# Two-map attention units: factor and epsilon column on GpSimd, the reciprocal on VectorE

## The reference

```python
logit_d = jnp.einsum('bqhcd,bkhcd->bchqk', dq_b, dk).astype(jnp.float32) * diff_scale
logit_d = jnp.where(allowed[:, None, None], logit_d + bias[:, None], NEG_INF_2)
p_d = jax.nn.softmax(logit_d, axis=-1)
attn_d = p_d[:, 0] - lam * p_d[:, 1]
o_d = jnp.einsum('bhqk,bkhd->bqhd', attn_d.astype(dv.dtype), dv)
o_d = _rms_norm(o_d, diff_sub_norm) * (1.0 - lam_init)
```

## Time and profile before

| | us |
|---|---|
| median of 3 runs | 1720.08 |
| lowest, highest run | 1719.74, 1720.19 |
| the profiled execution, device time | 1719.99 |
| its span in the profile | 1718.2 |
| first reciprocal of the two-map units, start | 1574.51 |
| last reciprocal of the two-map units, start | 1616.50 |

### The profile page before, as it was taken

The page is one execution under the profiler, slowest core; times in us unless marked ns, Lnnn a source line. Parts: engine busy times, 40 slices in busy tenths (PEclk is TensorE's granted clock), DMA queues, the critical chain, the costliest instruction groups (busy, mean ns, idle before and its releaser), DMA issues.

```text
span 1718.2 us, 22179 instructions
## 1 busy us (share of the span) xinstructions
PE 1685.8 (98%) x8825; PEld 1327.9 (77%) x8825; DVE 1029.0 (60%) x1675; ACT 633.9 (37%) x1001; POOL 61.5 (4%) x84
## 2 busy tenths in 40 slices
PE   7999999999999999999999999999999999999999
PEld 6888888787866678668888888888888866677687
DVE  5665444456977755448444457633554587878774
ACT  4222222231257851333222233312222567555730
POOL 0000000000012310000000000000000000002200
PEclk9999999999999999999999999999999999999999
DMA  6645433246300015133433233324332333402322
GB/s 205 204 162 180 135 99 90 69 122 204 94 2 2 2 40 158 61 86 84 107 94 97 85 104 98 91 85 121 88 96 83 100 105 99 127 15 61 100 74 74
DMA packets 233323, 167.60 MB, mean 98 GB/s; under 512 B 10436, under 2 KB 217532, under 8 KB 233092
## 3 DMA queue, kind: packets, MB, share of 16 engines
q1 hardware_dynamic: 230900, 161.98, 32.3%
q10 hardware_dynamic: 2320, 4.20, 0.7%
HBM read 156.31 MB, written 6.30 MB: 95 GB/s over the span
## 4 chain that ended last, share of the span: by engine, by line
PE 89%; DVE 6%; ACT 2%; issue 1%; SPq 1%; DMA 0%; POOL 0%; DVEq 0%; ACTq 0%
PE bank L1065 25%; PE bank L1066 25%; PE bank L1067 25%; PE turned L1314 3%; PE bank L1302 2%; PE bank L1340 2%; DVE bank L2122 1%; PE bank L1496 1%; ACT Pm L820 1%; PE bank L1404 1%; PE turned L1393 1%; PE bank L1622 1%; PE turned L1123 1%; DVE w_lo L1731 1%; SPq L458 0%
## 5 line engine op out<-in xcount | busy, mean ns | idle before, releaser
L1065 PE MATMUL bank<-h_hi,w_hi 128*128 128x512 f32 x1200 | 473.5, 395 | 2.8 <-DVE h_lo L1786 1.5
L1066 PE MATMUL bank<-h_lo,w_hi 128*128 128x512 f32 x1200 | 467.3, 389 | 0.0
L1067 PE MATMUL bank<-h_hi,w_lo 128*128 128x512 f32 x1200 | 467.3, 389 | 0.0
L650 ACT ACTIVATE w_hi<-w_raw 128x2048 fp32r<-128x2048 f32 (+3 forms) x134 | 236.9, 1768 | 495.7 <-PE bank L1067 494.9
L1731 DVE TENSOR_TENSOR w_lo<-w_raw,w_hi 128x2048 fp32r<-128x2048 f32 (+3 forms) x133 | 280.0, 2106 | 63.2 <-ACT w_hi L650 60.6
L1065 PEld LDWEIGHTS bank<-h_hi,w_hi 128*128 128x128 f32 x1200 | 225.3, 188 | 60.2 <-issue 11.8
L1067 PEld LDWEIGHTS bank<-h_hi,w_lo 128*128 128x128 f32 x1200 | 225.3, 188 | 47.4
L1066 PEld LDWEIGHTS bank<-h_lo,w_hi 128*128 128x128 f32 x1200 | 225.3, 188 | 46.6 <-issue 1.0
L1065 PE MATMUL bank<-u_hi,w_hi 128*128 128x512 f32 x352 | 137.1, 389 | 0.0
L1066 PE MATMUL bank<-u_lo,w_hi 128*128 128x512 f32 x352 | 137.0, 389 | 0.0
L1067 PE MATMUL bank<-u_hi,w_lo 128*128 128x512 f32 x352 | 136.9, 389 | 0.0
(11 more groups left out here) (428 smaller groups left out, 2282.1 us busy)
## 6 DMA issues: line engine op xcount, KB each, us to landing
w_raw<-in_w_in SPq DMA_DIRECT2D x28, 1024.0 KB, 5.4
w_raw<-in_ffn_w_gate SPq DMA_DIRECT2D x44, 512.0 KB, 4.0
w_raw<-in_ffn_w_up SPq DMA_DIRECT2D x44, 512.0 KB, 5.3
w_raw<-in_ffn_w_down SPq DMA_DIRECT2D x32, 704.0 KB, 4.7
ada_w<-in_ada_w SPq DMA_DIRECT2D x16, 768.0 KB, 6.5
w_raw<-in_w_in SPq DMA_DIRECT2D x19, 512.0 KB, 4.2
w_raw<-in_w_out SPq DMA_DIRECT2D x8, 1024.0 KB, 5.1
w_raw<-in_w_branch_nsa SPq DMA_DIRECT2D x8, 512.0 KB, 5.8
```

Source lines behind the costliest of these rows:

```text
L650: act.activation(w_hi[s % 2][:, 0:n], w_raw[s % 2][:, 0:n], ACT.Copy).then_inc(s_hi, 1)
L1065: pe.matmul(o, l[0], r[0], start=first, stop=False)
L1066: pe.matmul(o, l[0], r[1], start=False, stop=False)
L1067: return pe.matmul(o, l[1], r[0], start=False, stop=last)
```

## The change

The second and third instruction of `lam_sums` leave VectorE. GpSimd makes them in a new `lam_parts(v)`: first the epsilon column, as soon as the exponentials are there (`p_exp`), then the factor, as soon as VectorE has the reciprocal (`r1_ready`). Both count up `lam_ready`, and the weighing of a two-map unit waits for that instead of `sum_ready`. VectorE no longer waits behind the reciprocal for itself. The mask additions are put between: 0 to 2 as before, then for v = 16 to 31 `lam_parts(v)` and behind it addition v - 13 as long as there is one; these no longer wait for `p_ready`.

```diff
-            for i in range(16):
+
+            def bias_masked(i):
+
                 t = i % 4
                 pool.wait_ge(sem(f"bias_landed{t}"), 16 * (i // 4 + 1))
+                pool.tensor_add(bias[:, t, :], bias[:, t, :], hidden[t]).then_inc(sem("bias_ready"), 1)
+
+            def lam_parts(v):
+
+                u = U0 + v
+                sum0, r1, c1 = mstat[:, u % 2, 4:5], mstat[:, u % 2, 6:7], mstat[:, u % 2, 7:8]
+                pool.wait_ge(sem("p_exp"), u + 1)
+                pool.tensor_scalar(eps_sum(v), sum0, P * EPS, sum0, ALU.mult, ALU.mult).then_inc(sem("lam_ready"), 1)
+                pool.wait_ge(sem("r1_ready"), v - 15)
+                pool.tensor_scalar(c1, r1, sum0, neglam, ALU.mult, ALU.mult).then_inc(sem("lam_ready"), 1)
+
+            for i in range(3):
                 pool.wait_ge(sem("p_ready"), attended(U0 + 13 + i))
-                pool.tensor_add(bias[:, t, :], bias[:, t, :], hidden[t]).then_inc(sem("bias_ready"), 1)
+                bias_masked(i)
+            for v in range(16, len(UNITS2)):
+                lam_parts(v)
+                if v - 13 < 16:
+                    bias_masked(v - 13)
...
                 dve.wait_ge(sem("p_exp"), u + 1)
-                sum0 = mstat[:, u % 2, 4:5]
-                done(dve.reciprocal(mstat[:, u % 2, 6:7], mstat[:, u % 2, 5:6]))
-                tick(dve.tensor_scalar(mstat[:, u % 2, 7:8], mstat[:, u % 2, 6:7], sum0, neglam, ALU.mult, ALU.mult), "sum_ready")
-                tick(dve.tensor_scalar(eps_sum(v), sum0, P * EPS, sum0, ALU.mult, ALU.mult), "dve_seq")
+                tick(dve.reciprocal(mstat[:, u % 2, 6:7], mstat[:, u % 2, 5:6]), "r1_ready")
...
                 if kind == 0:
-                    dve.wait_ge(sem("sum_ready"), attended(u))
+                    dve.wait_ge(sem("lam_ready"), 2 * (v - 15))
                     tick(dve.scalar_tensor_tensor(p0, Pm[u % 2][:, 1, :], mstat[:, u % 2, 7:8], p0, ALU.mult, ALU.add), "p_ready")
```

More of the change, by code:

```diff
@@ L452, in build @@
         swap_used = {**{r: r - 1 for r in range(2, 10)}, **{r: r for r in range(12, 19)}, 19: 20}
+        UNITS2 = [(kind, h, t) for kind in (1, 0) for h in range(4) for t in range(NT)]
+        eps_sum = lambda v: col[:, G_MOD + v - 16:G_MOD + v - 15]
         attended = lambda u: u + 1 - sum(1 for w in UNITS[:u + 1] if w[0] is None)
@@ L610, in tick @@
             return count[name]
-        UNITS2 = [(kind, h, t) for kind in (1, 0) for h in range(4) for t in range(NT)]
-        eps_sum = lambda v: col[:, G_MOD + v - 16:G_MOD + v - 15]
         cq0, dq0, uq0, dkb0, ukv0 = (first_acc[n] for n in ("cq", "dqa", "uq", "dkb", "ukv"))
```

## The result

The changed kernel takes 1721.9 us (median of 20 runs, 1720.2 to 1722.95), the one before 1719.7 beside it (20 runs, 1718.2 to 1720.2): a ratio of 1.0014, 95% interval 1.0008 to 1.002. That is 2.2 us slower: the interval leaves out no change, but the difference is within the 0.2% that were set as the bound.

The account below looks back on a forecast made before the run. In the two-map stage the loop of VectorE and ScalarE, not TensorE, was taken to set the 2.77 us period. Terms 3.9-0.4+0.25+0.24, with roundings +4.1, on 1719.99 gave 1724.1 us; range 1716.3 to 1725.8.

Parts of the forecast that it names:

- main case: Either of two outcomes in the two-map units: addition first, +4.1 us, or weighing first, -3.5 us.
- The forecast case: Two-map units: the mask addition goes before the weighing; +4.1, 1724.1 us, own range 1722.5 to 1725.8, chance 0.57.
- TensorE's floor of 2.54: Two-map units: TensorE's own steps take 0.50, 0.98 and 1.06 us, so no unit can run below 2.54.
- Part 1: VectorE: second score operation moves from T+0.51 to T+0.08, weighing possible at T+0.68; T is the start of a unit's reciprocal.
- Part 2: GpSimd's one-column instructions: epsilon column hidden, factor 0.34 from T+0.26, no cost to the weighing; last unit +0.25.
- Part 3, the mechanism: Two-map units: the addition starts 0.08 before the weighing can, goes first, and the weighing ends about 0.53 behind it.
- Part 3, the start of the addition: GpSimd in two-map units: the mask addition starts right behind the factor, at T+0.60.
- the first score operation follows at +0.05: VectorE in two-map units: next score operation 0.05 behind the weighing's end, next reciprocal 0.62 later, period 3.07 for 2.77.
- The sum: Two-map stage: 3.9 for thirteen units, -0.4 for units 29 and 30, +0.25 end, +0.24 first unit; with roundings +4.1.
- Rival two: Two-map units: the weighing goes first and the addition waits; period 2.54 for 2.77, -3.5, 1716.5 us; chance 0.28.
- ring for GpSimd: GpSimd's unit if the weighing goes first: 0.34+0.34+1.27 and some 0.6 of waiting, 2.55 us.
- Rival three: No change: GpSimd bounds near 2.75 a unit, or the race varies; -1.5 to +1.5, taken as 1720; chance 0.15.

Follow-up runs that it names:

- e2: Changed kernel with mask additions 3 to 15 treating 8 of 512 columns, so part of the masks is missing; 1716.1 us, ratio 0.998.
- e8: Changed kernel with the epsilon column back on VectorE behind the reciprocal, additions 3 to 15 waiting for the next unit's second maximum; 1716.3 us, ratio 0.998.
- e3: Kernel before, with mask additions 3 to 15 waiting for the factor (sum_ready) instead of the weighing (p_ready); 1722.6 us, ratio 1.0016.
- e9: e8 without its added wait, so each mask addition stands directly behind the factor; 1721.9 us, ratio 1.0011.
- e6: Changed kernel with a one-column GpSimd memset between the factor and the mask addition; 1722.4 us, ratio 1.0014.
- e10: Changed kernel with one to four one-column memsets in turn between factor and addition in units 17 to 28, four in unit 16; 1723.3 us, ratio 1.0018.
- e5: Changed kernel with GpSimd's order factor, epsilon column, addition, and the weighing waiting for the factor alone; 1716.4 us, ratio 0.998.
- e11: Kernel before, with the epsilon column between reciprocal and factor in VectorE's order, GpSimd unchanged; 1718.0 us, ratio 0.9986.
- e1: Changed kernel with mask additions 3 to 15 waiting for p_ready again, so they stand behind the weighing; 1721.2 us, ratio 1.0008.

## Why the prediction was right, and where its size was off

The sign and the mechanism came as forecast, and the size at half: +2.2 for +4.1. That 1721.9 lies in the stated range of 1716.3 to 1725.8 says little, since that range reaches from one main case to the other. The forecast case had a range of its own, 1722.5 to 1725.8, and that one was missed by 0.6, on the low side. The result is also inside the 0.2% bound, which had the chance 0.37, and not in the likelier class, slower, with 0.46. The parts one by one:

- **TensorE's floor of 2.54: right.** e2 and e8 run at 2.540, and the score operation of VectorE waits for the scores there.
- **Part 1: right.** The second score operation starts at T+0.075 (said 0.08), and the weighing at T+0.67 (said 0.68), in twelve of twelve units.
- **Part 2: right in size, wrong for unit 16.** The factor starts at T+0.255 and takes 0.340, as said, extrapolated from 128 and 512 columns to one. The epsilon column is done before the factor could start in units 17 to 30 (it ends at T+0.10 at the latest). But in unit 16 the exponentials come late, it starts at T+0.02 and pushes the factor to T+0.38 and the weighing to T+0.76. There I had only the scaling in mind: 3.81 measured for 3.71. The last unit was foreseen: T+0.80 (said about 0.75), +0.30 for +0.25.
- **Part 3, the mechanism: right.** The addition goes first, the weighing waits for the whole of it and needs 0.55 more (said 0.53). e3 shows it without the moved instructions, e2 and e9 against e8 what it costs. That it goes first was given only a little better than even chances. It was no luck of the exact lead: it had 0.12 here and not the 0.08 that was worked out, but e6 and e10 show that it wins with 0.08, with less and with none. The argument by which I gave the addition the first turn, that it reaches its operands sooner since it has no per-partition operand to fetch, is borne out by e10, where it wins from 0.06 behind, and by e5, where a GpSimd instruction with such an operand loses from 0.03 behind. They differ in width and operation too, so that the fetching alone is the reason stays an argument.
- **Part 3, the start of the addition: 0.045 off.** I set it at the factor's end, T+0.60. It starts at T+0.555, 0.04 before the factor's row ends. That makes each period 0.045 shorter.
- **Part 3, the step that was mis-sized: "the first score operation follows at +0.05".** It starts 0.08 before the weighing's end. I had taken the 0.80 from the weighing's start to the next score operation for VectorE's own step. But it was a wait: before, the same operation starts some 0.16 behind the end of TensorE's scores, as the earlier trace rows would have shown one unit on (1589.39+1.13 = 1590.52; e11, with the same order there, has the wait in its rows). The step of VectorE itself stood in the earlier trace rows: the scaling starts at 1576.29, the weighing of before starts at 1575.62 and takes 0.75, so 0.08 before its end. I used that number for unit 16 and the other one for the twelve. This makes 0.13 a unit. In after alone this step and a wait for the scores can't be told apart, as its scores end 0.16 ahead too. But where they end 0.21 to 0.29 ahead the step is still 0.08 before the weighing's end: in all of e3's units 18 to 28, and in e10 (1587.64+1.83 = 1589.47 to 1589.39, with the scores done at 1587.97+1.13 = 1589.10). The trace of before has it once behind a weighing, in unit 17:

```profile
1578.79 0.75 DVE L2437 SCALAR_TENSOR_TENSOR Pm<-Pm,mstat 128x512 f32<-128x512 f32 x1
...
1579.46 0.69 DVE L2122 CUSTOM_DVE_ANT_0 bank<-bank,bias 128x512 f32<-128x512 f32 x1
```

- **The sum.** 0.13 and 0.045 bring 3.07 to 2.90; 2.907 was measured. Over the twelve units 17 to 28 that is 2.0 us, +1.6 for +3.6. The rest nearly cancels: unit 16 0.10 more, units 29 and 30 0.08 more, the end 0.05 more, the roundings 0.1 less. That is the whole way from +4.1 to +2.2.
- **Rival two** had its time right (1716.5; e2, e5 and e8 give 1716.1 to 1716.4) and its condition never comes true in after. Its ring for GpSimd came within 0.05 in e5 (2.60 for 2.55). **Rival three**: GpSimd is never the bound in after. It is in e1, where the addition waits for the weighing (2.946), and from unit 23 on in e5 (2.60).
- **The rule of the Trainium skill** (GPSIMD Engine Reference, Key points), that VectorE instructions with two SBUF inputs contend with GpSimd: the trace agrees (weighing 0.75 and 1.70), and the score operations, with one operand in a bank, keep 0.67 to 0.70 beside the addition. The page says contend; here it is a full exclusion of one by the other.

## What to carry to other kernels

When work moves to another engine, look first at what stands behind it there: the added instructions may be free, and the one that they bring forward may run into an instruction that it excludes, as the addition and the weighing do here. An order of the two queues that keeps the long instruction just behind the critical one can be worth more than the move itself (one wait is worth 5.6 us between e9 and e8, while the best of the whole kernels, e8, is 3.7 below the kernel before). And a distance between two starts is a cost of the engine only if nothing was waited for: look for another releaser, and for the same pair of instructions at a place where both were free to run.

## What the runs showed of the hardware

- A GpSimd addition of 128x512 with two SBUF inputs and a VectorE operation with two SBUF inputs don't share time. VectorE, if second, ends 0.55 behind GpSimd, whether it started 0.50 or 0.12 behind it (e3, after); GpSimd, if second, is 1.66 for 1.27 with a start 0.23 behind (e8). e3 and after differ by 0.38 in the start and by nothing in the end.
- Even one column waits: 0.82 for 0.264 (e5), for an instruction with a single input and a per-partition operand.
- The order of the starts in the rows does not by itself decide who goes first: the addition wins from 0.06 behind (e10), loses from 0.23 behind (e8).
- On GpSimd one column costs 0.264 with one per-partition operand and 0.340 with two. Between its instructions lie 0.10 (addition to epsilon, epsilon to factor in e1) or an overlap of 0.04 (factor to addition in after); each memset of 0.10 in its row moves what follows by 0.033 (e10).
